# Expert loop with a pipeline one block deeper on both sides, two HBM accumulators, and two semaphores per kind of weight load

## The reference, cut to what matters here

```python
def expert_block(args):                       # one block: up to 128 rows of one expert
    tok, e = args
    xb = h_pad[tok]                           # gather 128 token rows
    hid = jax.nn.silu(xb @ w_gate[e]) * (xb @ w_up[e])      # 1024 -> 256, twice
    return hid @ w_down[e]                    # 256 -> 1024

yb = lax.map(expert_block, (row_tok.reshape(n_blocks, MOE_BLOCK), block_e))
yb = yb.reshape(rows, d) * row_w[:, None]
return jax.ops.segment_sum(yb, row_tok, num_segments=t + 1)[:t]   # add to the tokens' rows
...
f = routed + shared_expert(h)
out = layer_norm(ALPHA * h + f, ln2_g, ln2_b)
```

## Time and profile before

| what | us |
|---|---|
| median of three runs | 1663.17 (1659.51 to 1664.15) |
| profiled execution, own time | 1656.49 |
| its span in the trace | 1654.8 |
| routing stage, about | 738 to 755 |
| expert loop, first up matmul to last | 768.03 to 1575.2 |
| final stage, from its first load | 1598.58 |
| PE busy over the span | 1337.8 (81%) |
| DVE busy | 1105.0 (67%) |
| ACT busy | 834.8 (50%) |
| POOL busy | 762.6 (46%) |

### The profile page before, as it was taken

The page is one execution under the profiler, slowest core; times in us unless marked ns, Lnnn a source line. Parts: engine busy times, 40 slices in busy tenths (PEclk is TensorE's granted clock), DMA queues, the critical chain, the costliest instruction groups (busy, mean ns, idle before and its releaser), DMA issues. The chain is left out here.

```text
span 1654.8 us, 22502 instructions
## 1 busy us (share of the span) xinstructions
PE 1337.8 (81%) x6080; PEld 1045.3 (63%) x6080; DVE 1105.0 (67%) x1480; ACT 834.8 (50%) x911; POOL 762.6 (46%) x811
## 2 busy tenths in 40 slices
PE   1397989879669999834999999999999988989920
PEld 1254656556357888723877787777777777778720
DVE  5930455262356777634888888788788777778858
ACT  2411101010543333204887887778777777778742
POOL 2477504410421433432566654566566334346634
PEclk9998989899879999866999999999999999999965
DMA  8223265272441221117888799989979999988643
GB/s 233 89 55 79 34 59 41 64 79 10 129 138 52 77 77 52 58 66 295 277 322 287 225 361 342 323 293 297 361 227 342 345 338 347 350 289 299 181 143 123
DMA packets 110606, 320.96 MB, mean 194 GB/s; under 512 B 30512, under 2 KB 61232, under 8 KB 85984
## 3 DMA queue, kind: packets, MB, share of 16 engines
q1 hardware_dynamic: 76256, 254.35, 46.3%
q0 software_dynamic: 27488, 63.16, 15.2%
q10 hardware_dynamic: 6816, 2.88, 0.9%
HBM read 282.87 MB, written 64.19 MB: 210 GB/s over the span
## 5 line engine op out<-in xcount | busy, mean ns | idle before, releaser
L1855 DVE TENSOR_TENSOR moe_up_l<-rt_raw_up,moe_up_h 128x2048 fp32r<-128x2048 f32 x158 | 361.3, 2288 | 44.3 <-ACT moe_up_h L1685 42.8
L1685 ACT ACTIVATE moe_up_h<-rt_raw_up 128x2048 fp32r x158 | 301.8, 1911 | 80.5 <-issue 62.7
L1768 POOL DMA_INDIRECT acc<-moe_y,moe_idx_s x77 | 152.2, 1976 | 282.6 <-DMA acc<-moe_y,moe_idx_s 258.7
L1799 PE MATMUL moe_p_gu<-moe_up_h,moe_x_h 128*128 128x512 f32 x616 | 252.1, 409 | 28.4 <-DVE moe_x_l L1864 28.4
L1876 DVE TENSOR_TENSOR moe_dn_l<-rt_raw_dn,moe_dn_h 128x2048 fp32r<-128x2048 f32 x77 | 176.7, 2295 | 105.4 <-ACT moe_dn_h L1726 105.4
L1799 PE MATMUL moe_p_gu<-moe_up_h,moe_x_l 128*128 128x512 f32 x616 | 244.3, 397 | 0.0
L1799 PE MATMUL moe_p_gu<-moe_up_l,moe_x_h 128*128 128x512 f32 x616 | 244.1, 396 | 0.0
L680 PE MATMUL mix_proj<-co_hT,co_win 128*128 128x384 f32 (+1 forms) x768 | 238.3, 472 | 6.5 <-PEq L102 6.5
L680 PEld LDWEIGHTS mix_proj<-co_hT,co_win 128*128 128x128 f32 x768 | 146.6, 192 | 94.6 <-issue 9.2
L1757 POOL DMA_INDIRECT moe_xg<-tok,moe_idx_g x80 | 139.0, 1737 | 63.6 <-POOL moe_idx_g L1754 63.6
L1726 ACT ACTIVATE moe_dn_h<-rt_raw_dn 128x2048 fp32r x77 | 148.3, 1926 | 22.4 <-DMA rt_raw_dn<-in_w_down_dram 11.9
(11 more groups left out here) (399 smaller groups left out, 2314.6 us busy)
## 6 DMA issues: line engine op xcount, KB each, us to landing
rt_raw_up<-in_w_gate_dram SPq DMA_DIRECT2D x64, 1024.0 KB
rt_raw_up<-in_w_up_dram SPq DMA_DIRECT2D x64, 1024.0 KB
rt_raw_dn<-in_w_down_dram SPq DMA_DIRECT2D x64, 1024.0 KB
co_win<-in_w_in_dram SPq DMA_DIRECT2D x16, 512.0 KB
resid<-trunk_x SPq DMA_DIRECT2D x9, 512.0 KB, 2.6
proj_res<-resid SPq DMA_DIRECT2D x9, 512.0 KB
...
```

What stands on the lines that cost most here:

```text
L1685: act.activation(up_h[:, par, half, :, :], raw_up[:, bass.ds(slot, 1), half, :, :].rearrange("p a k n -> p (a k) n"), ACT.Copy).then_inc(u ...
L1768: pool.indirect_dma_start(out=io.acc, in_=y[:, par, :], in_offset=None, out_offset=bass.IndirectOffsetOnAxis(ap=idx_s[:, par:par + 1], axi ...
L1799: mm = pe.matmul(p_gu[:, par, :].rearrange("p (a n) -> p a n", a=2), x, w, start=(i == 0), stop=(i == len(terms) - 1))
L1855: low = tt(up_l[:, par, half, :, :], raw_up[:, bass.ds(slot, 1), half, :, :].rearrange("p a k n -> p (a k) n"), up_h[:, par, half, :, :].b ...
```

## The change

Eight things change together.

1. The accumulator becomes two HBM tensors. Even blocks add to `io.acc[0]`, odd blocks to `io.acc[1]`, and `scatter` no longer waits for the scatter of the block before. (The scatter two blocks before, on the same tensor, is still waited for: y_out needs its `y` buffer back.)
2. `io.acc[1]` is filled with zeros in the trunk stage: a `blank` tile of 128x1024 that POOL sets, and nine DMAs of 512 KB from SP, ahead of the nine that keep the residual.
3. The final stage loads both accumulators (18 DMAs instead of 9) and DVE adds them, one 128x1024 addition per tile.
4. PE's turn becomes up(n), turn_hid(n-1), turn_x(n+2), down(n-2). ACT, DVE and POOL follow: hidden values and down weights of n-1, x of n+2, y and scatter of n-2, gather of n+4. The weights of up stay at n+2.
5. SP's order of loads stays down(e-3), gate_up(e), with the same slots; the down weights' low part of a block is now made one turn later.
6. Each kind of load has two semaphores, for even and odd experts; gate and up share one pair. A load waits for the load of its kind two experts before instead of one before.
7. The routing stage makes two more columns (how many loads of each parity must have landed) in place of the expert number; one more transpose and two more small DVE operations. ACT reads three table entries instead of two before the up and the down weights of a block, and waits on two semaphores of one kind each time.
8. Blocks 0 to 4 and the last two are emitted by hand; in the last two nothing is fetched or converted for blocks beyond the end. Before, that work was done for blocks past the end.

The diff, cut to its core:

```diff
+            for i in range(N_TILES):
+                sp.dma_start(io.acc[1][i * P:(i + 1) * P, :], blank[:, :]).then_inc(s_filled, 16)
...
@@ routing_stage, sync @@
+            sp.sem_inc(rt.up_in[1], 32)
+            sp.sem_inc(rt.down_in[1], 16)
             for e in range(UP_SLOTS):
-                for side, src, sem in ((0, io.w_gate, rt.gate_in), (1, io.w_up, rt.up_in)):
-                    if e:
-                        sp.wait_ge(sem, 16 * e)
+                if e >= 2:
+                    sp.wait_ge(rt.up_in[e % 2], 32 * (e // 2) + 32 * (e % 2))
+                for side, src in enumerate((io.w_gate, io.w_up)):
...
@@ expert_stage @@
+            body(early + (BEFORE - 1), 1, False)
+            body(early + BEFORE, 0, False)
...
-            def gate_up(e, slot, until):
+            def gate_up(e, slot, odd, until):
                 wait(sp, up_l_done, until)
                 sp.sem_inc(sp_go, 1)
-                for half, src, sem in ((0, w_g, gate_in), (1, w_u, up_in)):
-                    wait(sp, sem, e * 16)
-                    sp.sem_inc(sp_go, 1)
+                wait(sp, up_in[odd], e * 16 + 16 * odd)
+                sp.sem_inc(sp_go, 1)
+                for half, src in enumerate((w_g, w_u)):
...
@@ scalar, body @@
             silu(n, par)
-                x_high(n + 1, 1 - par)
-                slot = up_high_first(n + 2, par)
-                hid_high(n, par)
-                if not first:
-                    y_out(n - 1, 1 - par)
-                down_high(n, par)
-                up_high(n + 2, par, slot, 1)
+                if known(n, 1):
+                    hid_high(n - 1, 1 - par)
+                if more:
+                    x_high(n + 2, par)
+                    slot = up_high_first(n + 2, par)
+                if known(n, 1):
+                    down_high(n - 1, 1 - par)
+                if known(n, 2):
+                    y_out(n - 2, par)
+                if more:
+                    up_high(n + 2, par, slot, 1)
...
@@ gpsimd, scatter @@
-                wait(pool, added[1 - par], dma_count(n - 1, 1 - par) if not isinstance(n, int) or n else 0)
                 pool.sem_inc(go, 1)
-                pool.indirect_dma_start(out=io.acc, in_=y[:, par, :], in_offset=None,
+                pool.indirect_dma_start(out=io.acc[par], in_=y[:, par, :], in_offset=None,
...
@@ tensor, body @@
             up(n, par)
-                turn_x(n + 1, 1 - par)
-                if not first:
-                    down(n - 1, 1 - par)
-                turn_hid(n, par)
+                if known(n, 1):
+                    turn_hid(n - 1, 1 - par)
+                if more:
+                    turn_x(n + 2, par)
+                if known(n, 2):
+                    down(n - 2, par)
...
@@ vector, body @@
             hidden(n, par)
-                x_low(n + 1, 1 - par)
-                up_low(n + 2, par, (0,))
-                hid_low(n, par)
-                down_low(n, par)
-                up_low(n + 2, par, (1,))
+                if known(n, 1):
+                    hid_low(n - 1, 1 - par)
+                if more:
+                    x_low(n + 2, par)
+                    up_low(n + 2, par, (0,))
+                if known(n, 1):
+                    down_low(n - 1, 1 - par)
+                if more:
+                    up_low(n + 2, par, (1,))
...
@@ final_stage @@
+                sp.dma_start(x2[:, i, :], io.acc[1][i * P:(i + 1) * P, :]).then_inc(s_x[i], 16)
...
+                link(v.tensor_tensor(x[:, i, :], x[:, i, :], x2[:, i, :], ALU.add))
```

178 lines of the change are left out of this document (100 added, 78 removed).

## The result

On the same chip the kernel before took 1659.5 us (median of 5 runs) and the changed one 1650.4 us: ratio 0.9946, 95% interval 0.9926 to 0.9966. A second comparison later gave 0.9949 (0.9920 to 0.9979). The change is faster by 9 us, where I had forecast 34; the time lies inside my range, and the forecast of 1629 us is 21 us too low.

The account below looks back on a forecast made before the run. PE's idle time, from a scatter chain and an engine round, was taken to bound the loop, with DMA the floor in the middle stretch. Loop -42.4, head -1.5, tail -2, trunk 0, final stage +12 gave -34 us: 1629 us, range 1610 to 1656.

Parts of the forecast that it names:

- Both loops of the prediction: Expert loop: scatter chain, 11.08 us per block in the long run, and two-block engine round, 0.3 us per block; both go.
- The lengths I had forecast for the stretches: Expert loop: three stretches take 416, 236 and 76.5 us, sum 728.5 against 770.9, 42.4 us less.
- The step that failed: Long run: up loads leave about 7 us later, some 12 us remain against 11.0 of DMA work, so no hole.
- rival (c): Single-expert rows: up loads behind down(e-3) become the loop, 11.65 us a block in about 40 blocks; 1681 us, chance 0.08.
- Rival (a): Loop: scatters and gathers stay slow, POOL's 9.72 us round sets blocks outside the middle stretch; gain 21, 1650 us, chance 0.18.
- Rival (b): Loop: PE and DMA floors both met, 409 + 227 + 76 = 712 us, 59 less; 1612 us, chance 0.17.
- (d): Whole kernel: no change; stalls for gathered rows and weights leave 12 us gain, final stage eats it; about 1663, chance 0.07.
- The semaphores: Weight loads: waits by parity let two experts' loads of a kind be in flight; priced at nothing, DMA being full.
- Head: Routing stage and first blocks: routing ends 2.4 us earlier, up(3) comes 0.9 later; together -1.5 us, between -3 and +5.
- Tail: After the last up: two downs, last y 13.6 us behind that up's end instead of 15.6; -2 us, between -5 and +3.
- Final stage: Nine added DVE additions of 1.2 us, 10.8, plus about 1.2 for a second load; +12 us, between +9 and +18.
- Trunk: Stage before routing: zero fill by POOL's memset and nine DMAs fits where there is room; 0, at most +5 us.

Follow-up runs that it names:

- e3: The changed kernel with one accumulator, each scatter again waiting for the one before, no zero fill, second load or final addition: 1674.9 us, 1.0102 of before.
- e4: The kernel before with only the second accumulator added, old engine order and load semaphores kept: 1652.9 us, 0.9980 of before.
- e2: The changed kernel with ScalarE and VectorE converting down weights of n-1 ahead of the first up half of n+2: 1631.4 us, 0.9842 of before.
- e10: e2 with up weights ahead of x in the first two blocks, second accumulator added by DMA, bias additions four tiles behind: 1622.6 us, 0.9772 of before.
- e1: The changed kernel with SyncE's loads turned round, gate_up(e) ahead of down(e-3): 1656.9 us, 1.0005 of before.
- e6: e2 with each load also waiting for its kind's load one expert before, so no two are in flight: 1637.1 us, 0.9890 of before.

## Why the prediction was wrong

**What bound the kernel.** Both loops of the prediction were there and both went: POOL's 258.7 us of waiting for scatters and the alternation of 9.49 and 10.10 us. e3 and e4 show that neither pays much alone: with the scatter chain put back the deeper order takes 34.8 us more, and without that chain the old order gains 13.7. The lengths I had forecast for the stretches can be reached: e2 and e10 have 415 to 417, 235 and 78 us. The 336 GB/s of the middle stretch before were no limit of the transfers: block 31 of the changed kernel moved 421 GB/s over its 9.49 us, and e2's middle stretch ran at 346 GB/s.

**The step that failed** is that of the loads: "From issue to the moment when ACT needs them some 12 us are left, where DMA work of one expert and block takes 11.0. In the long run this makes no hole, because DMA has the next expert queued already ..." The wait was placed rightly (the up loads stand behind a down load that waits for a later down_low), but its length was taken from DMA work of 11.0 us, whereas ScalarE can start only 14.7 us after the last issue (1296.26 to 1310.93); the DMA view gives 13.7 us as the median from issue to landing of that load over the whole kernel. That the other loads in the same queue make the difference is my reading; no run takes them apart. And I asked only whether DMA would run dry, not what stands behind the waiting conversion on ScalarE. It is down_high of this turn: the late load delays not only the up weights but first of all the down weights, which had landed.

This is rival (c), term by term: I had 6.8 us from the landing to the down load's issue and 16.5 from there to the next landing, 11.65 us a block; the trace shows 7.05, 16.4 and 11.57. Its mark, ScalarE waiting for weights in the blocks of the long run, is there, and the DMA share fell to 0.96, though not under the 0.95 that I had set. What the rival had wrong is its extent: 15 blocks in a row and shorter pieces elsewhere (in blocks 22 to 25 and 39 to 41 PE stalls on down too), not 40 blocks. With its own point of decision at 15.4 us and its only measured row at 16.5, a chance of 0.08 was too little, and it should have been a term of the sum for the long run: 15 x (11.57 - 11.0) would have taken 8.6 us from the forecast gain. Its price had a slip as well: from block 0 to the end of the last up the kernel before takes 807 us (768.03 to 1575.2), and 801 to that up's start, not 799, so the rival's total should have been some 2 to 8 us lower than 1681.

**The order of ScalarE and VectorE** I had read for their lengths (8.93 and 8.71 us in a block of 9.49) and not for what each instruction may stand behind. Lengths were no limit: the full block at 1203.48 shows 8.15 on ScalarE and 8.75 on VectorE, and takes 9.49. The third table read cost nothing that shows. Rival (a) was wrong in its cause (POOL's scatter row grew from 1.98 to 3.11 us, see below; in e2 it is 3.18 us, and the middle stretch takes 235.5 us all the same), though its time, 1650, was the measured one; a time met by another mechanism proves nothing for that mechanism. Rival (b)'s floors (409, 227) were not reached by any kernel; (d) has no row for it, as PE's only wait for gathered rows that is left is the one for the very first (10.9 us, before 12.3).

**The clock** had no term in the sum. In the changed kernel six blocks of the middle stretch (49 and five of the long run's inside) show a granted clock of 0.87 to 0.90, each with a stall on down of 1.8 to 2.5 us in it; e2, whose stalls between up of block 3 and the last up are 1.4 us at most, shows 1.00 in all three stretches. But the rows show no loss by it in the long run. Two neighbouring pairs of its blocks, 52 with 53 and 54 with 55, the second with matmuls at the lower level:

```profile
1285.56:1308.88 23.32, 19.53 (x94) 15.93 (x92) 17.49 (x16) 16.13 (x16) 12.07 (x9) 1.00 0.98 331
1308.88:1332.37 23.49, 21.07 (x94) 17.06 (x93) 17.35 (x15) 16.12 (x16) 11.92 (x9) 0.93 0.93 324
```

PE is busy 1.5 us longer in the second pair and the pair takes 0.2 us more: the slower matmuls fill time in which PE would have waited, for PE is no link of the ring, whose round of about 23.5 us both pairs take. e1 agrees, though its order of loads is another: at a clock of 0.97 the inside of its long run takes 167.2 us, e2's at 1.00 takes 168.5. Outside the ring, as in block 49, a loss is possible and not measured.

**The semaphores**, priced at nothing: about 4 us to the good in e2's order (e6); in the changed kernel's own order they were not taken out.

**Head:** forecast -1.5, measured +4.2. The routing stage did end earlier: GpSimd's first instruction of the loop (it clears xg) starts 15.4 us after the stage's start instead of 17.6, 2.2 of the 2.4 forecast. But up(0) comes 8.1 us later from there, not 5.5: x, the wait of 0.96 us behind it, both halves on ScalarE and both on VectorE stand in a row, until 771.22. And of this only 1.7 us came back by up(3), where I had 4.6, because up(2) waits for conversions in its turn (VectorE's second half for it ends at 788.80):

```profile
788.90 0.47 PE L1829 MATMUL moe_p_gu<-moe_up_h,moe_x_h 128*128 128x512 f32 x1 [1.97 <-issue]
```

and block 2 takes 11.13 us at a clock of 0.85. Idle time of PE is no cover where what feeds PE is late by the same amount.

**Tail:** forecast -2, measured +2.9. I counted two downs after the last up; there are three, since down(n-2) stands behind up(n). ScalarE around it, after the end of the last up:

```profile
1555.77 1.91 ACT L1752 ACTIVATE moe_dn_h<-rt_raw_dn 128x2048 fp32r x1 [3.05 <-PE moe_p_dn L1841]
...
1569.55 1.02 ACT L1729 ACTIVATE moe_y<-moe_p_dn 128x1024 f32<-128x1024 f32 x1 [3.24 <-PE moe_p_dn L1841]
```

The conversion waits 3.05 us for the first of the three, which still reads its buffer, and the last y ends 18.5 us after the last up instead of 13.6: a down of about 3.2 us, and of the other two the first takes 5.0 us (1560.17 to 1565.17), as most of its matmuls run at the lower clock (0.50 from 1560.5 to 1564.0), 0.63 us each, where the last takes 3.0. The deeper pipeline has one block more to drain, and I had not written its list out.

**Final stage:** forecast +12, measured +15.5. The addition takes 1.21 to 1.23 us in eight of nine tiles, as I had said. The rest was under-sized: the first statistics come 9.5 us after the stage's first load where it was 5.4, 4.1 later (the first tile's two loads leave at 1578.37 and 1578.75, but 11 of the other 16 are issued before its addition starts at 1586.59, and from 1581.0 on the DMA share is 0.98), of which I had 2.4 with the addition itself; and in one tile the additions met, which the prediction had allowed for at up to 2.3 us:

```profile
1595.40 2.35 POOL L1967 TENSOR_TENSOR final_x<-final_x,final_lnb 128x1024 f32<-128x1024 f32 x1 [16.92 <-DVE final_x L1995]
1595.43 3.40 DVE L1999 TENSOR_TENSOR final_x<-final_x 128x1024 f32<-128x1024 f32 x1
```

The new addition met the first of GpSimd and took 3.40 us, 2.2 more, once and not in every tile.

**Trunk:** forecast 0; the routing stage started 2.6 us earlier than before, inside the spread given above, so nothing speaks against it.
